# Merging four stages, unrolling the down projection and reordering the final stage of a two-layer DiT block kernel

## The reference

```python
def rmsnorm(x, g):
    y = x32 * lax.rsqrt(jnp.mean(x32 * x32, axis=-1, keepdims=True) + EPS)
    return (y * g.astype(F32)).astype(x.dtype)
def modulate(xn, shift, scale): return xn * (1 + scale) + shift
...
    h = modulate(rmsnorm(x, norm_mix_g[l]), sh1, sc1)
    mix, mix_c = token_mixers(h, hc, w_in[l], ...)
    x = x + g1 * (mix @ w_out[l])
...
def moe_ffn(h, w_router, w_g, w_u, w_d):
    logits = (hf @ w_router).astype(F32)
    top_v, top_i = lax.top_k(logits, TOP_K)
    gates = jax.nn.softmax(top_v, axis=-1)
    order = jnp.argsort(flat_e)
    xs = hf[order // TOP_K]
    g = lax.ragged_dot(xs, w_g, sizes); u = lax.ragged_dot(xs, w_u, sizes)
    y = lax.ragged_dot(jax.nn.silu(g) * u, w_d, sizes)
    ...  # y times its gate, the two added for each token
```

## Time and profile before

| | us |
|---|---|
| median of three runs | 6039.61 |
| profiled execution, its own time | 6042.35 |
| its span in the trace | 6040.4 |
| PE busy | 5266.8 (87%) |
| PE weight loads | 3985.7 (66%) |
| DVE busy | 2766.7 (46%) |
| ACT busy | 2003.3 (33%) |
| POOL busy | 163.9 (3%) |

### The profile page before, as it was taken

The page is one execution under the profiler, slowest core; times in us unless marked ns, Lnnn a source line. Parts: engine busy times, 40 slices in busy tenths (PEclk is TensorE's granted clock), DMA queues, the critical chain, the costliest instruction groups (busy, mean ns, idle before and its releaser), DMA issues. The chain is left out here.

```text
span 6040.4 us, 61280 instructions
## 1 busy us (share of the span) xinstructions
PE 5266.8 (87%) x22972; PEld 3985.7 (66%) x22973; DVE 2766.7 (46%) x2881; ACT 2003.3 (33%) x1995; POOL 163.9 (3%) x239
## 2 busy tenths in 40 slices
PE   6899395699997969975675999999999999999994
PEld 3444174488886755433555888888888888888883
DVE  0220474311113332116623844599659654448466
ACT  1100111211112230002112634477547544447453
POOL 0000020000000000001101000000000000000001
PEclk7899697799998989987885999999999999999996
DMA  9111003221115441010036955599759755558576
GB/s 382 28 43 52 18 1 133 80 65 56 57 46 169 135 148 31 22 65 1 23 139 262 346 186 197 206 381 380 256 207 382 293 183 204 196 182 340 200 274 226
DMA packets 262623, 996.66 MB, mean 165 GB/s; under 512 B 40000, under 2 KB 112384, under 8 KB 175744
## 3 DMA queue, kind: packets, MB, share of 16 engines
q1 hardware_dynamic: 243200, 926.43, 41.7%
q0 software_dynamic: 13040, 49.29, 2.2%
q10 hardware_dynamic: 6288, 19.66, 0.8%
HBM read 911.68 MB, written 83.63 MB: 165 GB/s over the span
## 5 line engine op out<-in xcount | busy, mean ns | idle before, releaser
L1697 PE MATMUL ps<-moe_gate_up_hi,moe_xh 128*128 128x512 f32 x2464 | 963.0, 391 | 9.3 <-DVE moe_gate_up_lo L1849 9.3
L1697 PE MATMUL ps<-moe_gate_up_hi,moe_xl 128*128 128x512 f32 x2464 | 960.7, 390 | 0.0
L1849 DVE TENSOR_TENSOR moe_gate_up_lo<-moe_wst,moe_gate_up_hi 128x2048 fp32r<-128x2048 f32 x424 | 952.2, 2284 | 17.7 <-ACT moe_gate_up_hi L1780 17.7
L1697 PE MATMUL ps<-moe_gate_up_lo,moe_xh 128*128 128x512 f32 x2464 | 959.6, 389 | 0.0
L1780 ACT CAST moe_gate_up_hi<-moe_wst 128x2048 fp32r<-128x2048 f32 x424 | 791.1, 1924 | 0.1
L1862 DVE TENSOR_TENSOR moe_down_lo<-moe_wst,moe_down_hi 128x2048 fp32r<-128x2048 f32 x210 | 480.1, 2289 | 159.1 <-ACT moe_down_hi L1794 158.6
L1697 PEld LDWEIGHTS ps<-moe_gate_up_hi,moe_xh 128*128 128x128 f32 x2464 | 463.2, 188 | 106.8 <-DVE moe_gate_up_lo L1849 11.6
L1697 PEld LDWEIGHTS ps<-moe_gate_up_hi,moe_xl 128*128 128x128 f32 x2464 | 463.2, 188 | 96.9
L1697 PEld LDWEIGHTS ps<-moe_gate_up_lo,moe_xh 128*128 128x128 f32 x2464 | 463.3, 188 | 95.5
L1868 DVE TENSOR_TENSOR moe_a<-moe_sil,ps 128x512 f32<-128x512 f32 x210 | 143.4, 683 | 739.2 <-ACT moe_sil L1800 739.2
L1800 ACT ACTIVATE moe_sil<-ps 128x512 f32<-128x512 f32 x210 | 125.9, 600 | 982.5 <-PE ps L1697 982.4
(11 more groups left out here) (330 smaller groups left out, 6499.5 us busy)
## 6 DMA issues: line engine op xcount, KB each, us to landing
moe_wst<-in_moe_packed SPq DMA_DIRECT2D x634, 1024.0 KB, 6.7
ada_w<-in_ada_packed SPq DMA_DIRECT2D x24, 2048.0 KB, 26.4
down_wst<-in_ffn_w_down SPq DMA_DIRECT2D x66, 512.0 KB, 3.6
proj_w<-in_w_in SPq DMA_DIRECT2D x8, 2048.0 KB, 7.8
four_dft<-in_dft_seq SPq DMA_DIRECT2D x16, 1024.0 KB, 4.9
xs_d<-route_zero SPq DMA_DIRECT2D x1, 16384.0 KB, 50.8
moe_rows<-xs_d POOLq DMA_DIRECT2D x16, 1024.0 KB, 5.3
ys_d<-moe_y POOLq DMA_DIRECT2D x15, 1024.0 KB, 4.5
```

Of the source, the lines that this page charges most:

```text
L1697: x = nc.tensor.matmul(ps[:, 2 * (q % 2) + i, :], xx[:, k, t], w[:, q % 2, k, :], start=(k == 0 and j == 0), stop=(k == KD - 1 and j == 2))
L1849: nc.vector.tensor_tensor(gul[:, q % 2, k, :], wst[:, slot(n), :].rearrange("p (k n) -> p k n", k=4), guh[:, q % 2, k, :].bitcast(F32), AL ...
```

## The change

The 24 stages become 20.

1. *Stage ends.* The second meeting of all engines goes. GpSimd still clears the semaphores behind the Block, but the other engines go on; a stage's semaphores are freed for new use one stage later, and one last meeting closes the program.
2. *Norm and projection* are one stage in both layers. The order of units changes: all weights are first used for the context tokens (and conv and gates for the image too), then five of them are loaded a second time for the image tokens. Seven banks hold units, the eighth the sums of squares.
3. *Constants.* Two masks are stored once and not four times; the constants lose 696 columns, 356 KB.
4. *Zero fill and g2 store* go to the scan stage of layer 1, on SP, with the zeros made on GpSimd.
5. *Down projection.* No loops; rings of four for loads and three for parts; x per group; PE counts each block's last product in `summed`, DVE sums a group's blocks behind the second chunk of the next group; SP stores halves of a group.
6. *Norm, routing and experts* are one stage `phase_moe`. Logits come from sixteen products of 512 columns into four quarters of a bank and eight folding products, ranks from a scan on DVE and three products. Slots are written before the expert tables. Rows are turned and copied by ACT to a buffer that holds all of them, and the scatters wait only for the slots and their rows. SP loads expert weights as soon as the tables are there; the first two parts are split before the first unit's rows. The loop over units is otherwise the same, but for PE's wait for the tables.
7. *Final stage.* Each block of tokens has its own gather buffers, x has a ring of three and arrives in eight pieces, the row vectors come over ACT's queue, the first weighing is on ACT, and block n−1 is normalized behind block n's add.

```diff
     def __exit__(self, kind, value, trace):
+        if Phase.last is not None:
+            Phase.last.sem_stack.close()
         if kind is None:
             for s in self.sems:
                 self.nc.gpsimd.sem_clear(s)
-            self.nc.all_engine_barrier()
+        Phase.last = self
         self.stack.close()
...
-def phase_norm(nc, S, name, src, xT, hT, l, which, groups):
-def phase_project(nc, io, S, l, hT, FM, TM, ctx_out):
+def phase_norm_project(nc, io, S, l, src, hT, FM, TM, ctx_out):
+    NB, VAR = 7, 7
+    first = [n for n in ("qk", "t0", "t1", "t2", "four", "conv", "gates") if ctx_out or n not in only_out]
+    second = ["qk", "t0", "t1", "t2", "four"]
+    uses = [(i, n, GROUPS[:1]) for i, n in enumerate(first)]
+    uses += [(GATES - 1, "conv", GROUPS[1:]), (GATES, "gates", GROUPS[1:])]
+    uses += [(len(first) + i, n, GROUPS[1:]) for i, n in enumerate(second)]
...
+                variance(0)
+                variance(1)
                 seen = -1
                 for u, (i, kind, j, dst, a, n) in enumerate(units):
+                    if u == 0:
+                        pe.wait_ge(shifted, KD)
+                    if u == 2:
+                        variance(2)
+                    if u == image:
+                        pe.wait_ge(shifted, 3 * KD)
...
+                for g in range(2):          # ScalarE
+                    deviation(g)
+                    for k in range(KD):
+                        square(g + 1, k)
+                        shift(g, k)
+                evacuate(act, nc.scalar.copy, 0)
+                evacuate(act, nc.scalar.copy, 2)
+                deviation(2)
... # scan, layer 1
+                    sp.wait_ge(zeroed, 1)
+                    sp.dma_start(S["xs_d"].rearrange("(b p) d -> p b d", p=P), zero[:, :].unsqueeze(1).to_broadcast([P, 2 * (NUNIT + 1), D])).then_inc(filled, 16)
... # down projection
+    RING, PARTS = 4, 3
+    chunks = [(g, f) for g in range(len(GROUPS)) for f in range(NC)]
-                sp.dma_start(x[:, :, :], S["xT_d"]).then_inc(xl, 16)
+                for c, (g, f) in enumerate(chunks):
+                    t0, n = GROUPS[g]
+                    if c >= RING:
+                        sp.wait_ge(split, c - RING + 1)
+                    sp.dma_start(wst[:, c % RING, :], io["ffn_w_down"][0][f * P:(f + 1) * P, :]).then_inc(wl[c % RING], 16)
+                    sp.dma_start(ast[:, c % RING, :n], S["a_d"][:, f, t0:t0 + n]).then_inc(wl[c % RING], 16)
+                    if f == 8:
+                        sp.dma_start(x[:, :, t0:t0 + n], S["xT_d"][:, :, t0:t0 + n]).then_inc(xl[g], 16)
...
+                    if g and f == PARTS - 2:   # VectorE
+                        sums(g - 1)
+                sums(len(GROUPS) - 1)
... # experts
+                sp.wait_ge(tabled, 2)          # SyncE, ahead of the weight loads
...
+                pool.wait_ge(slots, 1)
+                for n in range(NX):
+                    pool.wait_ge(rv, n + 1)
+                    for i in range(2):
+                        nc.gpsimd.indirect_dma_start(
+                            out=S["xs_d"][:, :], out_offset=bass.IndirectOffsetOnAxis(ap=R["slot"][:, i, n:n + 1], axis=0),
+                            in_=trow[:, n, :], in_offset=None).then_inc(sc, 16)
+                pool.wait_ge(sc, 32 * NX)
...
+                def logit_parts(g):
+                    for kk in range(2):
+                        for j in range(4):
+                            x = nc.tensor.matmul(ps[32 * j:32 * j + 32, LPART + g, :], wr[:, 4 * kk + j, :],
+                                                 hT[:, 4 * kk + j, g * 512:(g + 1) * 512], start=(kk == 0), stop=(kk == 1))
... # final stage
-                    if n >= 2:
-                        pool.wait_ge(xr, n - 1)
+                def weigh(n):                  # ScalarE
+                    act.wait_ge(gl[n], 32)
+                    nc.scalar.activation(y[:, n, 0, :], y[:, n, 0, :], ACT.Copy, scale=R["gate"][:, 0, n:n + 1]).then_inc(first, 1)
...
+                    if n >= 1:                 # VectorE
+                        normed(n - 1)
```

More of the change, by code:

```diff
@@ L253, in _ @@
                 dve.wait_ge(mod_done, 1)
-def phase_norm(nc, S, name, src, xT, hT, l, which, groups):
[L258 to L312, removed]
-                    dve.wait_ge(sd_ready, g + 1)
-                    nc.vector.reciprocal(rstd[:, g % 2, :n], rstd[:, g % 2, :n]).then_inc(rst, 1)
-                    dve.wait_ge(rst, g + 1)
-                    for k in range(KD):
-                        nc.vector.scalar_tensor_tensor(
-                            out=xT[:, k, t0:t0 + n], in0=xT[:, k, t0:t0 + n], scalar=gmod[:, l, which, j, k:k + 1],
-                            in1=rstd[:, g % 2, :n], op0=ALU.mult, op1=ALU.mult).then_inc(scaled, 1)
@@ new lines, in _ @@
+                for k in range(KD):
+                    square(0, k)
+                for g in range(2):
+                    deviation(g)
+                    for k in range(KD):
+                        square(g + 1, k)
[3 more added lines that the diff above has]
+                deviation(2)
+                for k in range(KD):
+                    shift(2, k)
+                for u in range(4, len(units) + 8, 2):
+                    if u < len(units):
+                        evacuate(act, nc.scalar.copy, u)
+                    for j in range(4):
+                        if silu_at[j] in (u, u + 1):
+                            act.wait_ge(cv, j + 1)
+                            nc.scalar.activation(FM[:, 2 + j, :], y[:, j % 2, :], ACT.Silu).then_inc(silu_done, 1)
@@ L1370, in products @@
                             mm = nc.tensor.matmul(ps[:, d, :n], w[:, s, d * P:(d + 1) * P], aa[:, s, :n],
-                                                  start=(first and j == 0), stop=(last and j == 2))
-                    mm.then_inc(used, 1)
-                for g in range(3):
-                    over_chunks(pe, products, g)
+                                                  start=(f == 0 and j == 0), stop=(f == NC - 1 and j == 2))
+                        if f == NC - 1:
+                            mm.then_inc(summed, 1)
@@ L1787, in _ @@
                         gate_up_hi(0, q, j)
+                for s in range(4):
+                    rows_hi(0, s)
                 with act.Fori(0, NUNIT) as b:
```

716 lines of the change are left out of this document (409 added, 307 removed).

## The result

The changed kernel takes 5861.01 us (median of four, 5859.51 to 5862.69) against 6041.41 for the kernel before in the same session: a ratio of 0.9699, 95% interval 0.9686 to 0.9713. The forecast was 5867 in a range of 5830 to 5899. The profiled execution has a span of 5857.9, 182.5 less than before; the forecast had 172.9.

A forecast was written before the change was run, and what follows sets the result against it. TensorE was taken to bound three quarters of the program, so gains lie between its products: 0.8 + 25.8 + 25.6 + 47 + 37 + 10.7 + 26 = 172.9 us off the 6040.4 span, forecast 5867, range 5830 to 5899.

The forecast's parts named there:

- Expert head: Norm and routing up to the first expert product: with scatters and early weight loads sharing the DMA engines, 37 us gained.
- Rival B: Expert stage: the scatter keeps GpSimd's issue pace despite the weight loads, gain 62 instead of 37 us, whole 5842; chance 0.2.
- Down projection: Down projection stage: earlier first product, no stall between products and a shorter tail; 49 us by the sum, 47 taken.
- Projections: Norm and projection, both layers: context units start before the image tokens are normed; gains 25.8 us and 25.6 us.
- I leave it on both sides: Projection of layer 0: the slower clock of the first products costs 2.8 us, assumed the same before and after.
- Stage ends: The 14 stage ends otherwise unchanged: clears run beside the next stage, gaps of 15.4 us give 10.7, between 6 and 14.
- Final stage: Last stage: earlier DVE start and 5.6 us a block give 26.9 us, 26 taken, bounds 13 and 29.
- The first pair lands near 10.5: Final stage: the first pair of gathers lands about 10.5 us after the release, the first multiply ends at 11.6.
- The bound of 13: Final stage, low bound of the gain, 13 us: xT in eight pieces of 512 B packets lands late and sets the blocks' pace.
- Rival C: Rebuilt pieces give less, PE at 1.2 GHz in sparse context units: 36 us less, 5903 far end, 5895 middle; chance 0.18.
- Rival D: Expert loop: the weight stream becomes the bound in eight single-tile units, 144 us instead of 122, whole 6040 or more; chance 0.02.
- Rival E: Stage boundaries: all stages wait for GpSimd anyway, 11 us less gain, 5878; counted within the forecast's chance of 0.6.

The follow-up runs named there:

- the ends alone: The kernel before with only the new stage ends (no second meeting, semaphores freed a stage later), still 24 stages: 6019.2 against 6041.3 us, ratio 0.9963.

## Why the prediction was right

The mechanism was right in most parts, wrong in the final stage, and the sum was 9.6 us short of the profile's 182.5. That the total came so near is in part luck: the stage ends and the final stage missed by 9.1 and 8.2 us in opposite directions.

- *Expert head (37, measured 38.2).* Right step by step, and for its reason: the chance of 0.6 for "weights halve the scatter" against 0.2 for "it keeps GpSimd's pace" is borne out by 48.9 against 24.9 us. Rival B described what happens only when the weights wait.
- *Down projection (47, measured 49.3).* The working gave 49 and I took 47 for waits that hardly came: 1.2 us of PE's idle time waits for a block's sum.
- *Projections (51.4, measured 59.6).* Two terms were too dear: the third unit, by 1.2 us in layer 0 and 2.1 in layer 1, and the clock. "I leave it on both sides" was the step that failed: in the change PE is busy with sums just before its first units and doesn't pay the 2.8 (2.6 by the records of 256 columns). Conv's weights cost 0.9 in layer 0 where I had 1, and nothing in layer 1.
- *Stage ends (10.7, measured 19.8).* Some 15 of it are the ends and some 5 chance, so the term was 4 too low. About 2 of these are the scans: I let the four stages that GpSimd feeds lose their gap. The decays did (they gained nothing), the two scans gained 1.1 and 0.8. The norm before the up projection gave 3.1 at a gap of 1.1, and 2.9 with the ends alone; what the other 2 are stays open. The 1.5 of clock in the first Fourier stage is among the 5 of chance.
- *Final stage (26, measured 17.8).* Two terms failed. "The first pair lands near 10.5" was 14 and DVE began at 15.3 instead of 11.6, for the gathers now share the engines with x. (10.5 was also half a microsecond less than its own terms, 4.1 and the median of 6.9.) And I looked at how each block's own gather buffer frees the gathers, and not at what the new x ring of three waits for: the store, 8.8 us. Blocks of 5.16 instead of 5.6 gave 3.5 back. The bound of 13 named the 512 B packets of x, but as a delay of the transposes, not of a store behind them in the same queue.
- *Rival C* (clock in sparse stretches) had the sign wrong: the change keeps PE at full clock in its first units. It was also priced from a misread row: the 0.41 a record over 37 is a mean of 256 and 512 columns, and the first 16 records alone took 0.38 each. *Rival D* did not occur, the loop unit is 122.1 as before. *Rival E* is refuted by the run with the ends alone, 22 shorter.

The Trainium skill (DMA: Bandwidth & Descriptors, "Queues, rings and completion order") says that an engine alternates between queues by packets. The counts 582 and 581 agree, and the turns are of one of the profile's packets each, 8 KB against 4 KB. The final stage shows the price: the queue with 512 B packets moved 0.57 MB while the one with 4 KB packets moved 4.10, a seventh, and what stands behind it in its own queue waits with it.

## What to carry to other kernels

When a change starts transfers earlier, list what else is in flight then, with packet sizes: shares go by packets. A store that frees a buffer does not belong in a queue behind bulk loads of short packets. Value a removed stage gap at the gap, with the products that follow it at the lower clock as a possible extra (here 1.5 us in one of two stages), and when a stage's first products come straight from other PE work, count the slow start as saved. Before a difference of a few microseconds between two profiles is explained, look at how much the same code scatters. Let only those transfers run beside a critical one that its consumer needs at the same moment; four of ten loads were worth 14 us.

## What the runs showed of the hardware

- At the start of the Fourier stages, straight after the projection's products, PE's clock was full after 1.1 us without work in all 22 cases seen, full in three of four after 2.05 us, and lower in both after 2.77 us. The mean over 10 us from the Block's end was 0.83 of full where it fell after 2.05, and 0.66 and 0.83 after 2.77.
- Two queues shared the engines one packet each (582 and 581 packets in 15 us), with 424 GB/s for both together.
- Issuing eight loads of 512 KB in 512 B packets beside the gathers held SyncE for 34.3 us; two loads of 2 MB in 2 KB packets held it for 1.3.
- Sixteen scatters of 512 KB with nothing beside them land 24.9 us after the first issue, at GpSimd's pace of 1.27 us each; beside ten loads of 1 MB they take 48.9.
